# Two fused transformer blocks on one core: one product per mean, turned keys copied earlier, short attention pairs with two turn banks and two output banks

## What is computed

```python
def reference(...):
    x = first_block(x, ...)      # h = rms_norm(x); x += token_mixer(h); h = rms_norm(x); x += conv_ffn(h)
    return second_block(x, ...)  # h += hybrid_mixer(h); h += sqrelu_mlp(h); rmsnorm(h)

def rmsnorm(x, g):
    y = xf * lax.rsqrt(jnp.mean(xf * xf, axis=-1, keepdims=True) + EPS)

def nsa_attention(q, k, v, nsa_g, ...):      # 16 heads of 64, 2 key groups
    o = gc[..., 0:1] * o_c + gc[..., 1:2] * o_s + gc[..., 2:3] * o_w   # compressed, selected, window

def gla_chunked(q, k, v, log_a, strict):     # 4 heads, chunks of 64 tokens, both directions
    q_dec = q * jnp.exp(b)
    k_inv = k * jnp.exp(-b)
    A = jnp.where(mask, jnp.einsum('bhnid,bhnjd->bhnij', q_dec, k_inv), 0.0)
    contrib = jnp.einsum('bhncd,bhnce->bhnde', k * jnp.exp(b_last - b), v)
```

## Time and profile before

| | |
|---|---|
| median of 3 runs | 3191.18 us (3187.76 to 3192.89) |
| profiled execution | 3190.32 us |
| its span, first to last instruction | 3188.5 us |
| granted TensorE clock, mean | 0.987 |
| TensorE busy | 3095.8 us, 97% |
| VectorE busy | 1478.8 us, 46% |
| ScalarE busy | 1203.7 us, 38% |
| GpSimd busy | 392.5 us, 12% |
| HBM | 50 GB/s over the span |
| share of the chain of waits | TensorE 91%, VectorE 3%, ScalarE 3%, issue 2% |

### The profile page before, as it was taken

One profiled execution on the slowest core, in us unless ns is written; L12 is line 12 of the kernel. 1 busy time (PEld: TensorE's weight loads), 2 busy tenths in 40 slices (PEclk: granted clock), 3 DMA queues, 4 the chain that ended last, 5 costly groups with the idle time before them and its releaser, 6 DMA issues.

```text
span 3188.5 us, 43075 instructions
## 1 busy us (share of the span) xinstructions
PE 3095.8 (97%) x16992; PEld 2549.5 (80%) x16992; DVE 1478.8 (46%) x2247; ACT 1203.7 (38%) x1848; POOL 392.5 (12%) x616
## 2 busy tenths in 40 slices
PE   9999997899999999999999999999999999999998
PEld 6888887788988878888888878557778788888887
DVE  6652356657763435524533632565454322223234
ACT  4651136877773232312311331465442311212123
POOL 0110006655542000000000000120010000000000
PEclk9999997999999999999999999999999999999999
DMA  3222220000004211111111131001102111111112
GB/s 140 82 78 79 106 86 8 2 1 2 1 2 159 85 47 46 53 46 46 53 46 46 53 130 47 21 2 34 40 14 99 46 46 47 51 46 46 53 46 73
DMA packets 52204, 168.05 MB, mean 53 GB/s; under 512 B 9072, under 2 KB 12272, under 8 KB 51680
## 3 DMA queue, kind: packets, MB, share of 16 engines
q1 hardware_dynamic: 41088, 125.96, 11.8%
q0 software_dynamic: 10976, 40.15, 3.5%
HBM read 143.54 MB, written 16.78 MB: 50 GB/s over the span
## 4 chain that ended last, share of the span: by engine, by line
PE 91%; DVE 3%; ACT 3%; issue 2%; POOL 0%; DMA 0%; SPq 0%; ACTq 0%; DVEq 0%; POOLq 0%
PE PS L226 70%; PE PS L862 3%; PE PS L848 3%; PE PS L248 2%; PE PS L832 2%; PE PS L833 2%; PE PS L1627 2%; PE PS L1654 1%; PE PS L1639 1%; PE PS L883 1%; PE PS L2287 1%; ACT P_SHORT L931 1%; PE PS L874 1%; ACT PT L941 0%; PE PS L318 0%
## 5 line engine op out<-in xcount | busy, mean ns | idle before, releaser
L199 ACT CAST WHI<-RAW 128x1024 fp32r<-128x1024 f32 x219 | 230.3, 1052 | 1345.1 <-PE PS L226 1325.3
L204 DVE TENSOR_TENSOR WLO<-RAW,WHI 128x1024 fp32r<-128x1024 f32 x219 | 268.4, 1226 | 1002.1 <-ACT WHI L199 1001.7
L226 PE MATMUL PS<-HLO,WHI 128*128 128x512 f32 x2160 | 666.7, 390 | 0.0
L226 PEld LDWEIGHTS PS<-HLO,WHI 128*128 128x128 f32 x2160 | 406.6, 188 | 85.2
L226 PE MATMUL PS<-X_HI,WHI 128*128 128x512 f32 x1504 | 467.0, 392 | 4.5 <-DVE W L339 2.2
L226 PE MATMUL PS<-X_HI,WLO 128*128 128x512 f32 x1504 | 464.0, 390 | 0.0
L226 PEld LDWEIGHTS PS<-X_HI,WHI 128*128 128x128 f32 x1504 | 282.0, 188 | 66.6 <-DVE W L339 2.7
L226 PEld LDWEIGHTS PS<-X_HI,WLO 128*128 128x128 f32 x1504 | 283.0, 188 | 59.1
L226 PE MATMUL PS<-HID_HI,WHI 128*128 128x512 f32 x832 | 256.3, 389 | 1.2 <-DVE WLO L204 1.2
L226 PE MATMUL PS<-HID_LO,WHI 128*128 128x512 f32 x832 | 256.2, 389 | 0.0
L226 PE MATMUL PS<-HID_HI,WLO 128*128 128x512 f32 x832 | 256.1, 389 | 0.0
(11 more groups left out here) (353 smaller groups left out, 4650.2 us busy)
## 6 DMA issues: line engine op xcount, KB each, us to landing
RAW<-in_w SPq DMA_DIRECT2D x219, 512.0 KB, 3.2
X<-in_x SPq DMA_DIRECT2D x8, 512.0 KB, 8.5
Q<-QN POOLq DMA_DIRECT2D x32, 128.0 KB, 2.7
merged<-W POOLq DMA_DIRECT2D x8, 512.0 KB, 3.1
W<-gate POOLq DMA_DIRECT2D x8, 512.0 KB, 4.1
W<-merged POOLq DMA_DIRECT2D x8, 512.0 KB, 4.8
X<-in_x POOLq DMA_DIRECT2D x8, 512.0 KB, 9.8
x_kept<-X POOLq DMA_DIRECT2D x8, 512.0 KB, 8.5
```

The source lines that it names most:

```text
L199: nc.scalar.copy(WHI[:, slot, :], RAW[:, slot, :]).then_inc(w_hi, 1)
L204: nc.vector.tensor_tensor(WLO[:, slot, :], RAW[:, slot, :], WHI[:, slot, :].bitcast(F32), ALU.subtract).then_inc(w_lo, 1)
L226: last = nc.tensor.matmul(o[:, half], w[:, slot, cols], x(k)[:, half], start=(k == 0 and w is WHI and x is hi), stop=(done and k == kcs - ...
```

## The change

Three things change.

1. **Means.** VectorE adds the eighth square too (`dve_acc(n, KC - 1)`), and `pe_mean` multiplies ACC alone: two fp32 matmuls in place of four, for the norms 0 to 3. The counts of `acc_done` become 8 per norm. The fifth norm only has its counts renumbered.
2. **Turned keys.** In `act_z2` the copies of turned keys 0 and 1 move ahead of the duplicates of the same step, and those of keys 2 and 3 ahead of the weight split `act_split(u + 2)`.
3. **Short attention pairs.** Turned chunks use two banks in place of three (`bank_at`, `wait_turn_bank`: a chunk waits for the copy of the last one in its bank). The freed bank at 3T + 512 holds the outputs of odd pairs (`out_ps`), and `pe_cmp_values(m)` waits for the low part of pair m - 2, no longer of m - 1. On ScalarE `act_out_hi(m - 1)` moves from ahead of the copies to between the exps of the two heads; on VectorE `dve_out_lo(m - 1)` moves from behind the first head's shifts to behind the second head's. Long pairs keep the order and the banks of before; the first chunk in bank 3T + 512 waits for `o_free` of 32.

```diff
-            dve.wait_ge(acc_done, 7 * n + k)
+            dve.wait_ge(acc_done, 8 * n + k)
 def pe_mean(pe, n):
-        pe.wait_ge(acc_done, 7 * n + 7)
-        for first, src in ((True, ACC), (False, SQ[1])):
-            if not first:
-                pe.wait_ge(sq_done, 8 * n + 8)
-            for half in (slice(0, 512), slice(512, T)):
-                last = nc.tensor.matmul(SIDE[0][:, half], ONES[:, :], src[:, half], start=first, stop=not first)
-        last.then_inc(mean_done, 1)
+        pe.wait_ge(acc_done, 8 * n + 8)
+        halves(pe, SIDE[0], ONES[:, :], ACC).then_inc(mean_done, 1)
...
-    T_PS = [PS[:, c:c + 512] for c in (2 * T, 2 * T + 512, 3 * T + 512)]
-    O_PS = [PS[:, 3 * T + P * i:3 * T + P * i + P] for i in range(2)]
+    T_PS = [PS[:, 2 * T + 512 * i:2 * T + 512 * i + 512] for i in range(2)]
...
+    TURN_BANKS = (T_PS[0], T_PS[1], C0_PS)
+        bank = len(bank_at) % 2 if m < PAIRS_SHORT else (bank_at[-1] + 1) % 3
+        bank_before.append(in_bank[bank])
...
+    def out_ps(m):
+        return PS[:, 3 * T + 512 * (m % 2):3 * T + 512 * (m % 2) + P] if m < PAIRS_SHORT else \
+            PS[:, 3 * T + P * (m % 2):3 * T + P * (m % 2) + P]
+    def wait_turn_bank(pe, c):
+        if bank_before[c] is not None:
+            wait_copied(pe, bank_before[c])
+        elif bank_at[c] == 2:
+            pe.wait_ge(o_free, PAIRS_SHORT)
...
 def pe_turn(pe, m, i):
-        if c >= 3:
-            wait_copied(pe, c - 3)
+        wait_turn_bank(pe, c)
 def pe_cmp_values(pe, m):
-        if m:
+        if m > PAIRS_SHORT:
             pe.wait_ge(o_free, m)
+        elif m >= 2:
+            pe.wait_ge(o_free, m - 1)
 def act_attention(act):
-            if m:
+            if m >= PAIRS_SHORT:
                 act_out_hi(act, m - 1)
             for i in b[0]:
                 act_copy(act, m, i)
             if ahead:
                 if len(b) == 1:
                     act_exp(act, 2 * ahead, 0)
                 act_exp(act, 2 * ahead, 1)
+            if 0 < m < PAIRS_SHORT:
+                act_out_hi(act, m - 1)
             if ahead:
                 act_exp(act, 2 * ahead + 1, 0)
                 act_exp(act, 2 * ahead + 1, 1)
 def dve_attention(dve):
-            if m:
+            if m >= PAIRS_SHORT:
                 dve_out_lo(dve, m - 1)
...
                 dve_shift(dve, 2 * ahead + 1, 0)
                 dve_inverse(dve, 2 * ahead)
                 dve_shift(dve, 2 * ahead + 1, 1)
+            if 0 < m < PAIRS_SHORT:
+                dve_out_lo(dve, m - 1)
 def dve_residual(dve, u0, n, x, old, ready):
             ...
+        dve_acc(dve, n, KC - 1)
 def act_z2(act, units):
             j = jobs_before(u)
+            if u == U_RG + 1:
+                act_turned_keys(act, 2)
+                act_turned_keys(act, 3)
             act_split(act, u + 2)
             if u > units[0]:
                 act_turned_values(act, u - 1)
-            if u == U_RG + 1:
-                act_turned_keys(act, 2)
-                act_turned_keys(act, 3)
+            if u == U_RG - 1:
+                act_turned_keys(act, 0)
+                act_turned_keys(act, 1)
             if U_QG <= u < U_RG:
...
-            if u == U_RG - 1:
-                act_turned_keys(act, 0)
-                act_turned_keys(act, 1)
@@ first norm, VectorE's list
                 dve_acc(dve, 0, k - 1)
+        dve_acc(dve, 0, KC - 1)
         dve.wait_ge(consts[1], ALL_REST)
```

More of the change, by code:

```diff
@@ L756, in build, with count_copy @@
     MASKED = {m + 1: s for m, s in SELECTED.items()}
+    N_SHORT = 4 * 2 * HPG
+    PAIRS_SHORT = N_SHORT // 2
+    TURN_BANKS = (T_PS[0], T_PS[1], C0_PS)
     turned_at, used_at, c_turned_at, c_scored_at = [], [], [], [None]
-    by_dve, nth_copy = [], []
-    copies = [0, 0]
-    def count_copy(dve):
+    by_dve, nth_copy, bank_at, bank_before = [], [], [], []
+    copies, in_bank = [0, 0], [None, None, None]
+    def count_copy(dve, m):
+        bank = len(bank_at) % 2 if m < PAIRS_SHORT else (bank_at[-1] + 1) % 3
         copies[dve] += 1
@@ L765, in count_copy @@
         nth_copy.append(copies[dve])
+        bank_at.append(bank)
+        bank_before.append(in_bank[bank])
+        in_bank[bank] = len(bank_at) - 1
     n_u = 0
@@ L861, in pe_use @@
                 for e in range(2):
-                    last = nc.tensor.matmul(O_PS[m % 2][half_of(e), :], (VS, VW)[branch][:, kt, g],
+                    last = nc.tensor.matmul(out_ps(m)[half_of(e), :], (VS, VW)[branch][:, kt, g],
                                             PT[u % 8][:, 2 * x + e, :], start=False,
@@ L878, in pe_cmp_scores @@
         qt, g = s // 2, s % 2
-        if s and c_scored_at[s] >= 3:
-            wait_copied(pe, c_scored_at[s] - 3)
-        out = T_PS[c_scored_at[s] % 3] if s else C0_PS
+        if s:
+            wait_turn_bank(pe, c_scored_at[s])
+        out = turn_ps(c_scored_at[s]) if s else C0_PS
         for h in range(HPG):
@@ L940, in act_copy @@
             act.wait_ge(pv_done, u - 7)
-        nc.scalar.copy(PT[u % 8][:, 0:n, :], T_PS[c % 3][:, 0:P * n].rearrange("p (x q) -> p x q", q=P))\
+        nc.scalar.copy(PT[u % 8][:, 0:n, :], turn_ps(c)[:, 0:P * n].rearrange("p (x q) -> p x q", q=P))\
             .then_inc(pt_copied, 1)
@@ L948, in act_cmp_scores @@
         act.wait_ge(c_bias, s)
-        nc.scalar.copy(EC[:, :, :], T_PS[c % 3].rearrange("p (h n) -> p h n", n=HEAD)).then_inc(pt_copied, 1)
+        nc.scalar.copy(EC[:, :, :], turn_ps(c).rearrange("p (h n) -> p h n", n=HEAD)).then_inc(pt_copied, 1)
     def act_cmp_copy(act, s):
@@ L953, in act_cmp_copy @@
         act.wait_ge(t_done, c + 1)
-        nc.scalar.copy(PCT[s % 2][:, :, :], T_PS[c % 3].rearrange("p (x q) -> p x q", q=P)).then_inc(pt_copied, 1)
+        nc.scalar.copy(PCT[s % 2][:, :, :], turn_ps(c).rearrange("p (x q) -> p x q", q=P)).then_inc(pt_copied, 1)
     def act_cmp_exp(act, s):
@@ L967, in act_out_hi @@
         for e in range(2):
-            nc.scalar.copy(out_of(O_HI, m, e), O_PS[m % 2][half_of(e), :]).then_inc(o_hi, 1)
+            nc.scalar.copy(out_of(O_HI, m, e), out_ps(m)[half_of(e), :]).then_inc(o_hi, 1)
     def act_attention(act):
@@ L1142, in dve_out_lo @@
             dve.wait_ge(o_hi, 2 * m + e + 1)
-            last = nc.vector.tensor_tensor(out_of(HLO, m, e), O_PS[m % 2][half_of(e), :],
+            last = nc.vector.tensor_tensor(out_of(HLO, m, e), out_ps(m)[half_of(e), :],
                                            out_of(O_HI, m, e).bitcast(F32), ALU.subtract)
```

28 lines of the change are left out of this document (13 added, 15 removed).

## The result

| | before | after |
|---|---|---|
| median of the runs, us | 3192.02 (3187.76 to 3192.89, 4 runs) | 3155.97 (3154.76 to 3157.05, 4 runs) |
| ratio, 95% interval | | 0.989 (0.9872 to 0.9907) |
| profiled execution, its span, us | 3190.32, 3188.5 | 3156.06, 3154.3 |
| TensorE, ScalarE, VectorE busy, us | 3095.8, 1203.7, 1478.8 | 3083.4, 1204.1, 1482.3 |

The change makes the kernel 36 us faster, 1.1%; the forecast was 3155, with a range of 3142 to 3174. Set side by side, the two traces give the place: -1.0 us up to the first product behind norm 0, -17.3 in attention (first product of pair 0, at 483.46 and 482.36, to the product behind the last pair), -1.8 at norm 1, -1.8 at norm 2, -9.3 at the turned keys, -1.3 from there past norm 3.

The account below looks back on a forecast made before the run. TensorE, busy for 97% of the span, was taken to bound the kernel. Means -6.2, turned keys -9.3 and short pairs -20 sum to -35.5 us, from 3190.3 to 3154.8, forecast 3155; range 3142 to 3174.

Parts of the forecast that it names:

- Means: Norms 0 to 3: half of each 3.45 us mean goes, less a new 0.65 us wait at norm 0; -6.2 us.
- Turned keys: Key copies moved earlier: two TensorE waits of 3.2 us go, with clock time behind them; -9.3 us.
- Short pairs: Attention, 484 to 684 us: TensorE's 27.0 us of waits for VectorE's low part go, less new waits; -20 us.
- Clock, forecast -4: Short pairs, 500 to 580 us: granted clock 0.88 costs about 7 us busy; 4 of it comes back.
- Pair 32: Its first chunk takes the odd outputs' bank and waits for the low part of pair 31; +1.6 us.
- latecomers and two banks: Short pairs: new waits for ScalarE and VectorE, +5 us; chunks waiting for copies in two banks, +5.4 us.
- ScalarE's side: Short pairs counted by ScalarE's idle time: of 50 us idle 29 stay, so -21 us.
- the waits only move: Rival 1: ScalarE and VectorE already set attention's pace; attention 0 to -8, total 3171 us; chance 0.14.
- both engines run free: Rival 2: ScalarE's waits for minima and probabilities vanish too; attention -30, total 3145 us; chance 0.15.
- The slower case: Rival 3: TensorE stops 2.0 us at third turns of 16 pairs; attention +28.5, total 3203 us; chance 0.05.
- The copies of the keys did fit: Against rival 4: key copies miss ScalarE's hole, duplicates up to 1.9 us late; keys 0, total 3164; chance 0.06.
- The clock stays low: Rival 5: short stops at two banks keep the attention stage at clock 0.88; attention -6, total 3169 us; chance 0.05.

Follow-up runs that it names:

- the base: Kernel before with the means' edit and both key edits, attention stage as before; 3174.35 us, ratio 0.9939 to the kernel before.
- e3_att: Changed kernel with the means' and keys' edits undone, so the attention edit alone; 3174.58 us, ratio 0.9951 to the kernel before.
- f0_whole: The changed kernel as it is, timed again beside the parts; 3155.01 us against 3192.85 for the kernel before, ratio 0.9886.
- e1_means: Kernel before with the means' edit alone: VectorE adds the eighth square, one product pass per mean; 3185.37 us, ratio 0.9985.

## Why the forecast was right, and which term was off

The mechanisms came as forecast; that the total agrees within 1 us is partly luck. In the traces the three terms come to -32.5 in place of -35.5, the attention being 2.7 short, and a step of the clock elsewhere, -1.7, which no term had, made up for over half of that. The medians, -36, lie another 2 us off the traces' -34.

- *Means*, -6.2. Norm 0: forecast 1.07 with a new wait of 0.65; it came to 0.98 with 0.50 of later start, and the mean takes 1.97 there, not 1.72. Norms 1 and 2: forecast 1.72, steps 1.77 and 1.75. Norm 3's own record is of that length too, but the stretch around it, -1.3, holds other things. In all -5.9. Right.
- *Turned keys*, -9.3. Came as -9.31 in the changed kernel and -9.32 alone. With only the first half moved, clock of about 1.5 us comes back at the second in the one trace; that the halves depend on each other isn't shown by that, as old stages differ by 3 us among themselves.
- *Short pairs*, -20: came as -17.3, -16.7 and -17.3 in three traces. From TensorE's side the sum was -19.0. Line by line: the 27.0 us of waits, forecast gone, 0.2 left. Clock, forecast -4: -4.2, in pairs 8 to 15, and 1.2 us were lost again at pair 16. Against the base, whose clock there was 0.93 and not 0.86, those pairs would show 0.6 us in place of 4.2, so this term agrees by the execution that it was taken from. Pair 32, forecast +1.6: +1.35 (1.5 in idle time). The two entries for latecomers and two banks, +5 and +5.4: TensorE's other waits rose from 8.6 to 18.6 us, of which pair 32 is 1.7, and the broken turns add 3.0 busy, so 8.3 + 3.0 = +11.3 for 10.4. The waits of the turns were forecast by their idle time, 4.0 + 1.4; by pairs 16 to 30 they are 6.6 - 2.9 = 3.7 idle and 3.0 busy, 6.7. **The term that was off** is the last step, from -19 to -20 because of ScalarE's side with -21; the two sides came to -17.4 and -18.2. There 7 us were set for TensorE as the slower one at four chunks; ScalarE's waits for turns are 12.9, while those for the scores, set to stay at 11, are 6.0. ScalarE's idle time from pair 0 to 33 fell by 18.2 us (214.84 - 162.40 to 197.47 - 163.19).
- *The rivals.* That the waits only move (3171) and that both engines run free (3145) are both wrong; the waits for PT copies came to 11.5 us (8.0 + 3.5) where over 12 was to refute the forecast, and to 13.0 in e3_att, whose gain was the same: that bound was set too low. The slower case would have needed stops of 1.2 us in 16 pairs; TensorE's stops before turns are 0.6 on the mean (8.0 over 14). The copies of the keys did fit.
- *The clock stays low* (3169). In the stretch of the many stops the changed kernel shows:

```profile
568.00:664.00 96.00, 89.28 (x867) 74.83 (x864) 60.92 (x201) 80.86 (x204) 61.16 (x75) 1.00 0.01 2
```

  The rule that spoke for it, in the Trainium skill, page "TensorE: Matmul & The Clock Gate", section "A second HAM failure mode: psum-queue depth-cycling", is told there of bf16 matmuls of 512 columns and doesn't show here, with fp32 turns of 128: in pairs 16 to 30, 13 stops before turns for copies, with two banks, go with a clock of 0.99 and, in f0_whole, of 1.00. With two turn banks and one output bank the clock did stand at 0.83 from 500 to 580 us; but kernels with three turn banks stand there at 0.80 (e1_means) to 0.90, so the number of banks doesn't decide it.

## What to carry to other kernels

When one engine waits at one place for a buffer that another engine reads late, a second buffer can be worth much of that wait, and moving the reader in its list some on top; here 15 us and 6.7 for waits of 27 us. Price the bank that is taken away for it too, and count at each new stop not only the idle time but the overlap of matmuls that breaks there, 0.2 to 0.26 us here. Look at the granted clock behind each wait that goes: for the keys it gave a third of the gain, for attention up to a quarter. And take the stage's length before from more than one trace if its clock moves: here one and the same old stage took 213 to 220 us, as much as most of the pieces are worth.

## What the hardware did that was not expected

One and the same kernel differs by steps of 1.3 to 1.9 us at the same few places from execution to execution. Two executions of the changed kernel, the profiled one of the result and that of f0_whole, around short stops of TensorE at norm 1 and in later stages (columns as above):

```profile
1160.00:1164.00 4.00, 1.77 (x8) 1.20 (x7) 2.36 (x2) 1.34 (x2) 0.00 (x0) 0.99 0.10 18
1164.00:1168.00 4.00, 4.00 (x12) 3.09 (x12) 2.99 (x3) 1.88 (x2) 0.00 (x0) 0.59 0.32 119
1876.00:1881.00 5.00, 2.70 (x17) 2.36 (x17) 4.55 (x4) 2.06 (x2) 0.00 (x0) 1.00 0.38 126
1990.00:1998.00 8.00, 4.37 (x9) 1.97 (x8) 3.06 (x4) 1.63 (x2) 0.47 (x2) 0.71 0.20 66
```

```profile
1160.00:1164.00 4.00, 2.71 (x12) 1.90 (x11) 1.47 (x2) 1.05 (x1) 0.00 (x0) 1.00 0.00 0
1164.00:1168.00 4.00, 3.06 (x13) 2.55 (x14) 2.65 (x3) 2.18 (x2) 0.00 (x0) 1.00 0.38 135
1876.00:1881.00 5.00, 3.05 (x11) 2.76 (x12) 4.16 (x4) 1.81 (x2) 0.00 (x0) 0.67 0.46 147
1990.00:1998.00 8.00, 4.37 (x16) 2.44 (x14) 3.35 (x5) 1.47 (x2) 0.70 (x3) 1.00 0.20 66
```

Behind a stop of the same length (2.2 us within these 8 us in both) the clock is at the lower of its two levels, 1.2 GHz, for a part of the next 4 us (mean 0.59) in one execution and not in the other. At the second place it is the other way round, at the third as at the first. Each such fall costs about 1.6 us; a handful of them, met or missed, is as large as the spread of a kernel's runs. So a single trace's total shouldn't be set against another's below some 5 us, while a stage without such a stop repeats to 0.1 us: the turned keys, where no stop is left, came to -9.29 to -9.32 in ten executions of nine kernels. With the stop left in, as in e1_means, the two pieces behind it took 5.11 + 7.94 us in place of the 3.61 + 6.44 of the earlier trace rows, 3 us more for the same 3.2 us of waiting, and the stage is as long in e3_att. So half of that edit can look like nothing.
